# A hybrid decoder step: row scales by matmul in place of transpose, and one sample-state step in one window

## The chip, the cores and the metric
The kernel runs on one core of a Trainium2 chip. The metric is the device time of one execution in microseconds (us). The core has five engines with their own instruction streams, which meet only through semaphores: PE (TensorE, the matmul array; PEld is its weight load), DVE (VectorE), ACT (ScalarE), POOL (GpSimd) and SP (SyncE, which issues most transfers). Each stream is executed in order.

## The reference: what is computed
Two layers over a prompt of 2048 tokens of width 1024, and, apart from them, one decoding step for 8 samples that have a state each. A layer is:

```
h = rmsnorm(x) ; z = h @ w_in                 # one projection, columns split by branch
GLA:       S = diag(alpha) S + k^T v ; o = q S  ; o = rmsnorm_per_head(o) * silu(gate)
Retention: S = gamma_h S + k^T v     ; o = q S  ; o = groupnorm_per_head(o) * silu(gate)
y = x + concat(o_gla, o_ret) @ w_out
```

A final rmsnorm follows. For the prompt both recurrences are computed in chunks, as masked products of q, k and v with a carried state; for the 8 samples they are one step of the recurrence. Returned are both outputs and the four sets of states. Everything is f32.

## The kernel before
The prompt is cut in 4 blocks of 512 tokens for each of 2 layers, so there are 8 blocks n = 0 to 7. A block is cut in 4 token tiles of 128 (t), and its work in windows w = 1 to 32 of one weight slot each. Windows come in units u = (w - 1) // 4 of four slots: unit 0 is retention's q and k, 1 its v, 2 its gate, 3 is GLA's q and k, 4 its v, 5 its gate, and 6 and 7 are the output projection. Weights and activations are split in a high and a low part (`w_hi`, `w_lo`, `h_hi`, `h_lo`, `m_hi`, `m_lo`), and a product is three passes of the array: high by high, high by low, low by high. These are line L697, 24 for each window, 6 into each of four PSUM banks q = 0 to 3. ACT rounds a weight slot to `w_hi` (L257), POOL subtracts it from the slot to get `w_lo` (L264).

The order on each engine is the order in which the program text issues it. Each engine runs through the same windows, and between the products of window w and those of w + 1 come the small steps that the code assigns to window w. A wait on a semaphore holds everything behind it on that engine.

The steps that the change touches:

- **The row scales** (`scale_rows`, PE, line L383). The next block's activations are loaded already transposed, tokens along the free axis, and need the factor 1/rms of each token along that axis. POOL makes the factors `xrs` (128 x 4, L570). For each token tile, PE takes a column of `xrs`, repeated to 128 x 128, against the identity, and so writes a tile in which each row holds the 128 factors into the bank called ATT. DVE's `next_scaled` (L394) multiplies the activations by norm weight and that bank. It is done for n = 0 at the very start and for n = 1 to 3 in window 27 of the block before. Layer 2 doesn't use it.
- **The GLA state of the samples** (`sample_state_gla`, DVE, L1377). In the second block of each layer (n = 1 and n = 5, called kind 1) the states of the 8 samples lie in `ss`, two halves p of 128 x 1024. `sample_decay_gla` (L1371) multiplies both halves by alpha in window 15; the outer products k v lie in `v_b` (the first half of it is a part of the buffer `region`). Adding them is one `tensor_tensor` for each half, the first in window 16 and the second in window 17. The second signals the step V_SS[1]. PE's `sample_outputs(1)` (L802), after the products of window 17, waits for it, and so does SP, which stores the states in window 19.

The neighbours of that step on DVE, in windows 16 and 17, are `mixed(0, t)` (L1619, which waits for ACT's affine step L1229 of the same tile; that one in turn waits for a `m_lo` of POOL, L627) and the GLA q and k of window 17: L1699 twice and L1702 twice, which read the four PSUM banks of unit 3, multiply them by the decay factors and write them to `q_t` and `k_t`. Each of these frees a bank. PE's products of window 17, the first of unit 4, wait for bank q (`free_bank`, semaphore `qk_gla`) before they write it.

Windows of PE and of the other engines are not in step: DVE's steps of window 17 start as soon as the banks of unit 3 are complete, which is when PE is at the end of its window 16.

Of the kernel before, what the change touches and what calls it, by code (L numbers as in the profile page):

```python
# [25 lines left out]
TOK = 128  # L26
# [15 lines left out]
V_SP, V_SS = (8, 10), (9, 15)  # L42
# [18 lines left out]
def build(nc, d):  # L61
    f32, f32r, u8 = mybir.dt.float32, mybir.dt.float32r, mybir.dt.uint8
    ALU, ACT = mybir.AluOpType, mybir.ActivationFunctionType
    ctx = ExitStack()
    with ctx:
        def sb(name, shape, dt=f32):
            return ctx.enter_context(nc.sbuf_tensor(name, shape, dt))
# [51 lines left out]
        xrs = sb("xrs", [128, TPB])  # L119
        yrs = sb("yrs", [128, TPB])  # L120

        ident = sb("ident", [128, 128])
# [15 lines left out]
        ss = sb("ss", [128, 2, DECB, DV])  # L138
        ss_row = ss[:, :, :, :].rearrange("p i b n -> p (i b n)")
        v_b = (region[:, 1024:2048].rearrange("p (b n) -> p b n", b=DECB), sb("v_b", [128, DECB, DV])[:, :, :])  # L140
# [21 lines left out]
        P, ATT, OB, ST, X = bank[0:4], bank[4], bank[5], bank[6], bank[7]  # L162
# [213 lines left out]
        def scale_rows(pe, m):  # L376

            if m > 0:
                pe.wait_ge(rstd_x.sem, rstd_x.at(m, 1))
            for t in range(TPB):  # L380
                if m == 0 and t % 2 == 0:
                    pe.wait_ge(first_rs, t // 2 + 1)
                i = pe.transpose(ATT[:, TOK * t:TOK * t + TOK], xrs[:, t:t + 1].to_broadcast([128, 128]), ident[:, :])  # L383
            i.then_inc(ht_ps.sem, KT)

        def next_scaled(vec, m, k):
# [864 lines left out]
        def _(vec):  # L1251
# [8 lines left out]
            def step(i):  # L1260
                i.then_inc(s_v.sem, 1)
# [42 lines left out]
            for l in range(DEPTH):  # L1304
                def body(l, n, kind):
                    def done(k):
                        vec.wait_ge(s_v.sem, s_v.at(l, k))
# [15 lines left out]
                    def sample_gate():  # L1323
                        vec.wait_ge(gl_s.sem, gl_s.at(l, 3))
                        step(vec.scalar_tensor_tensor(al[:, :], X[:, 144:160], 0.0, gt[:, :], ALU.min, ALU.subtract))

                    def sample_q_ret():

                        vec.wait_ge(zt_sb.sem, zt_sb.at(l, 1))
                        apart()  # L1330
                        step(vec.stream_shuffle(rot[:, :, :], z_t[:, 0:4, :], [(p + 16) % 32 for p in range(32)]))
                        done(3)
                        vec.tensor_scalar(z_t[:, 0:2, :], z_t[:, 0:2, :], small[:, 0:1], None, ALU.mult)
                        step(vec.tensor_scalar(z_t[:, 2:4, :], z_t[:, 2:4, :], small[:, 2:3], None, ALU.mult))
                        done(4)
                        vec.scalar_tensor_tensor(rot[:, 0:2, :], rot[:, 0:2, :], small[:, 1:2], z_t[:, 0:2, :], ALU.mult, ALU.add)
                        step(vec.scalar_tensor_tensor(rot[:, 2:4, :], rot[:, 2:4, :], small[:, 3:4], z_t[:, 2:4, :], ALU.mult, ALU.add))
                        done(5)
                        for hh in range(2):
                            r = slice(64 * hh, 64 * hh + 64)  # L1340
                            vec.tensor_copy(q_s[r, 0, :, :, hh], rot[r, 0:2, :])
                        step(vec.tensor_copy(k_s[:, 0, :, :], rot[:, 2:4, :]))

                    def sample_q_gla():
                        vec.wait_ge(zt_sb.sem, zt_sb.at(l, 3))
                        for hh in range(2):
                            r = slice(64 * hh, 64 * hh + 64)
                            vec.tensor_scalar(q_s[r, 1, :, :, hh], z_t[r, 8:10, :], DK ** -0.5, None, ALU.mult)
                        step(vec.tensor_copy(k_s[:, 1, :, :], z_t[:, 10:12, :]))

                    def sample_product(g):

                        vec.wait_ge(v_in.sem, v_in.at(l, 64 * g + 64))
                        for p in range(2):
                            i = vec.tensor_tensor(v_b[p], v_b[p], k_s[:, g, p, :].unsqueeze(2).to_broadcast([128, DECB, DV]), ALU.mult)
                        step(i)

                    def sample_state_ret():

                        done(V_SP[0])  # L1360
                        vec.wait_ge(state_in, l * 64 + 32)
                        for p in range(2):
                            i = vec.scalar_tensor_tensor(ss[:, p, :, :], ss[:, p, :, :], small[:, 4 + p:5 + p], v_b[p], ALU.mult, ALU.add)
                        step(i)

                    def sample_decay_gla():

                        vec.wait_ge(state_in, l * 64 + 64)
                        vec.wait_ge(al_s.sem, al_s.at(l, 1))
                        s2 = ss[:, :, :, :].rearrange("p i b n -> p (i b) n")  # L1370
                        step(vec.tensor_tensor(s2, s2, al[:, :].unsqueeze(2).to_broadcast([128, 16, 128]), ALU.mult))  # L1371

                    def sample_state_gla(p):

                        if p == 0:
                            done(V_SS[1] - 1)
                        i = vec.tensor_tensor(ss[:, p, :, :], ss[:, p, :, :], v_b[p], ALU.add)  # L1377
                        if p == 1:
                            step(i)

                    def sample_moments(g):

# [55 lines left out]
                    def sample_residual(u):  # L1438
                        vec.wait_ge(slot_used, n * SLOTS + (4 * (6 + u) + 5 + RING))
                        c = slice(128 * u, 128 * u + 128)  # L1440
                        step(vec.tensor_tensor(xs[:, c], OB[:, 0:128], xs[:, c], ALU.add))

                    def sample_work(w):
                        if kind == 0:
                            if w == 4:
                                sample_gate()
                            if w == 8:
                                sample_q_ret()
                            if w == 19:
                                sample_q_gla()  # L1450
                        if kind == 1:
                            if w == 9:
                                sample_product(0)
                            if w == 10:
                                sample_state_ret()
                            if w == 13:
                                sample_product(1)
                            if w == 14:
                                sample_moments(0)
                            if w == 15:  # L1460
                                sample_decay_gla()
                            if w == 17:
                                sample_normed(0)
                            if w == 18:
                                sample_affine(0)
                            if w == 19:
                                sample_moments(1)
                            if w == 21:
                                sample_normed(1)
                            if w == 23:  # L1470
                                sample_affine(1)
                                sample_mixed()
                            if w == 29:
                                sample_residual(0)
                        if n % NBLK == 2:
                            if w == 8:
                                done(V_X1)
                                sample_stats(l + 1)
                            if w == 14:
                                sample_mean(l + 1)  # L1480
# [186 lines left out]
                    for w in range(1, SLOTS):  # L1667
                        if kind == 0 and w == 2:
                            clear_states()
                        if w in (3, 4):  # L1670
# [7 lines left out]
                            for p in range(2):  # L1678
                                i = vec.tensor_tensor_scan(half_la[:, p, :], keep[:, :], half_la[:, p, :], 0.0, ALU.mult, ALU.add)
                            i.then_inc(scan_sb.sem, 1)  # L1680
                            vec.wait_ge(scan_sb.sem, scan_sb.at(n, hf + 1))
                            for sgn in range(2):
                                i = vec.tensor_scalar(nb[:, :, sgn, 2 * hf:2 * hf + 2], la[:, :, 256 * hf + MID:256 * hf + 256:TOK], (2.0 * sgn - 1.0) / TAU, None, ALU.mult)
# [3 lines left out]
                        if w == 8:  # L1687
# [3 lines left out]
                            for p in range(2):  # L1691
                                i = vec.tensor_tensor(cc[:, p, 0:TPB - 1], ex[:, p, 0, TOK - 1:BLK - TOK:TOK], em[:, 1:TPB, p, 0], ALU.mult)
# [12 lines left out]
                        if w == 20:  # L1705
                            vec.wait_ge(sret_sb.sem, sret_sb.at(n, 5))
                            vec.wait_ge(sgla_sb.sem, sgla_sb.at(n, 0))
                            for p in range(2):
                                c = slice(128 * p, 128 * p + 128)
                                i = vec.tensor_scalar(s_mid[:, c], s_gla[:, c], em[:, 0, p, 0:1], None, ALU.mult)  # L1710
# [23 lines left out]
                        for g, first in ((0, 9), (1, 21)) if kind == 0 else ():  # L1734
                            t = w - first
# [5 lines left out]
                                norm(g, t - 2)  # L1741
                            if 1 <= t <= TPB:
                                stats(g, t - 1)
                        if kind == 1 and w in (16, 17):
                            sample_state_gla(w - 16)
                        if 14 <= w < 18:
                            mixed(0, w - 14)
                        if w == (2 if n == 0 else 1 if n < NBLK - 1 else 18) and n < LAST:
# [54 lines left out]
                    if n % NBLK == 2:  # L1803
                        sample_norm(l + 1)

                blocks(l, body)


# [116 lines left out]
```

## Time and profile before
| | |
|---|---|
| median of 3 runs | 1724.93 us (1724.77 to 1725.31) |
| the profiled execution | 1724.93 us |
| its span, first to last instruction | 1722.9 us |
| PE busy | 1701.6 us, 99% |
| DVE busy | 942.0 us, 55% |
| POOL busy | 842.1 us, 49% |
| ACT busy | 657.6 us, 38% |

The profile is of one execution. A row of a timeline gives start and length in us; rows of the same form that follow each other are merged (x2, x4), with the time from the first start to the last end. Starts of one engine can lie before the end of its instruction before, because an engine overlaps them: a matmul of PE with 512 columns takes 0.39 us, but the next one starts 0.23 us after it. For PE the distance between two starts is therefore the price of an instruction, and not its length. In square brackets stands the idle time ahead of an instruction and who ended it. An instruction's length on DVE or POOL includes the time for which it was held off after its issue.

### The profile page before, as it was taken

The numbers are of one execution on the slowest core, as the hardware profiler recorded it, in microseconds if no ns is written. First come the engines' busy times: TensorE is split into PE (matmuls) and PEld (weight loads), VectorE is DVE, ScalarE is ACT, GpSimd is POOL, SyncE is SP. The second block draws the span as 40 slices with busy tenths as digits, with TensorE's granted clock in tenths as the row PEclk, the third lists the DMA queues.
The fourth block names the chain that finished last, engine by engine and source line by source line (L and its number), as shares of the span: only waits on it lengthen the run. The fifth ranks groups of instructions, "written<-read, shape, count | busy, mean of one in ns | idle before, by whom it ended". The sixth has DMA issues, their size and how long they took to land.

```text
span 1722.9 us, 26529 instructions
## 1 busy us (share of the span) xinstructions
PE 1701.6 (99%) x10266; PEld 1401.0 (81%) x10266; DVE 942.0 (55%) x2284; ACT 657.6 (38%) x1287; POOL 842.1 (49%) x661
## 2 busy tenths in 40 slices
PE   6999999999999999999999999999999999999998
PEld 4888878888788887888878888788888888878886
DVE  7643566746555174464454535759556464584454
ACT  4433334333344234343452424434244343443322
POOL 4444345654455444464444544547445464454635
PEclk9999999999999999999999999999999999999999
DMA  7422356434442244322452224563244322442224
GB/s 259 135 65 84 100 207 197 147 111 145 161 137 84 86 135 159 117 86 83 136 168 88 74 74 149 184 178 128 74 150 159 111 76 85 134 157 80 86 86 140
DMA packets 100189, 215.97 MB, mean 125 GB/s; under 512 B 12896, under 2 KB 15328, under 8 KB 100064
## 3 DMA queue, kind: packets, MB, share of 16 engines
q10 hardware_dynamic: 73872, 134.51, 23.7%
q1 hardware_dynamic: 26192, 79.76, 14.2%
q8 instruction: 81, 1.33, 0.3%
q14 instruction: 44, 0.36, 0.1%
HBM read 192.34 MB, written 21.89 MB: 124 GB/s over the span
## 4 chain that ended last, share of the span: by engine, by line
PE 99%; DMA 1%; DVE 0%; issue 0%; ACT 0%; ACTq 0%; POOLq 0%; POOL 0%; SPq 0%
PE bank L697 82%; PE bank L972 2%; PE bank L1013 2%; PE bank L978 2%; PE bank L760 1%; PE bank L956 1%; PE bank L939 1%; PE bank L918 1%; PE bank L373 1%; PE bank L880 1%; PE bank L922 1%; PE bank L718 0%; PE bank L989 0%; PE bank L770 0%; PE bank L897 0%; PE bank L662 0%
## 5 line engine op out<-in xcount | busy, mean ns | idle before, releaser
L264 POOL TENSOR_TENSOR w_lo<-w_stage,w_hi 128x512 fp32r<-128x512 f32 x264 | 360.9, 1388 | 352.3 <-ACT w_hi L257 352.3
L697 PE MATMUL bank<-h_hi,w_hi 128*128 128x512 f32 x1024 | 410.2, 401 | 3.7 <-DVE h_lo L361 3.7
L697 PE MATMUL bank<-h_lo,w_hi 128*128 128x512 f32 x1024 | 400.4, 391 | 0.0
L697 PE MATMUL bank<-h_hi,w_lo 128*128 128x512 f32 x1024 | 400.2, 391 | 0.0
L264 POOL TENSOR_TENSOR w_lo<-ss,w_hi 128x512 fp32r<-128x512 f32 x164 | 216.5, 1341 | 232.4 <-ACT w_hi L257 232.4
L257 ACT ACTIVATE w_hi<-w_stage 128x512 fp32r<-128x512 f32 x264 | 152.6, 624 | 352.4 <-PE bank L697 311.0
L697 PEld LDWEIGHTS bank<-h_hi,w_hi 128*128 128x128 f32 x1024 | 192.7, 188 | 53.9 <-issue 7.2
L697 PEld LDWEIGHTS bank<-h_hi,w_lo 128*128 128x128 f32 x1024 | 192.8, 188 | 41.5
L697 PEld LDWEIGHTS bank<-h_lo,w_hi 128*128 128x128 f32 x1024 | 193.0, 189 | 37.0
L697 PE MATMUL bank<-w_hi,m_hi 128*128 128x512 f32 x512 | 203.6, 398 | 0.0
L697 PE MATMUL bank<-w_hi,h_hi 128*128 128x512 f32 x512 | 202.7, 396 | 0.0
L697 PE MATMUL bank<-w_lo,m_hi 128*128 128x512 f32 x512 | 199.6, 390 | 0.0
L697 PE MATMUL bank<-w_hi,m_lo 128*128 128x512 f32 x512 | 199.6, 390 | 0.0
L697 PE MATMUL bank<-w_hi,h_lo 128*128 128x512 f32 x512 | 199.6, 390 | 0.0
L697 PE MATMUL bank<-w_lo,h_hi 128*128 128x512 f32 x512 | 199.4, 390 | 0.0
L257 ACT ACTIVATE w_hi<-ss 128x512 fp32r<-128x512 f32 x164 | 94.6, 623 | 212.9 <-PE bank L697 177.0
L264 POOL TENSOR_TENSOR w_lo<-v_b,w_hi 128x512 fp32r<-128x512 f32 x84 | 110.5, 1336 | 124.3 <-ACT w_hi L257 124.3
L570 POOL TENSOR_TENSOR rstd<-var,half 128x4 f32<-128x4 f32 x64 | 66.4, 1038 | 131.3 <-DVE var L1594 68.0
L697 PEld LDWEIGHTS bank<-w_hi,h_hi 128*128 128x128 f32 x512 | 96.3, 188 | 20.2 <-issue 1.2
L697 PEld LDWEIGHTS bank<-w_hi,h_lo 128*128 128x128 f32 x512 | 96.1, 188 | 20.4
L697 PEld LDWEIGHTS bank<-w_hi,m_lo 128*128 128x128 f32 x512 | 96.1, 188 | 20.2
L697 PEld LDWEIGHTS bank<-w_hi,m_hi 128*128 128x128 f32 x512 | 96.2, 188 | 20.1 <-issue 0.4
(221 smaller groups left out, 2279.8 us busy)
## 6 DMA issues: line engine op xcount, KB each, us to landing
w_stage<-in_w_slots ACTq DMA_DIRECT2D x264, 256.0 KB, 3.0
ss<-in_w_slots ACTq DMA_DIRECT2D x164, 256.0 KB, 2.9
v_b<-in_w_slots ACTq DMA_DIRECT2D x84, 256.0 KB, 3.0
region<-in_x_prompt SPq DMA_DIRECT2D x32, 512.0 KB, 4.2
xn<-in_x_t SPq DMA_DIRECT2D x16, 512.0 KB, 4.3
out_acts<-region SPq DMA_DIRECT2D x16, 512.0 KB, 3.5
xn<-out_acts SPq DMA_DIRECT2D x16, 512.0 KB, 3.8
region<-out_acts SPq DMA_DIRECT2D x16, 512.0 KB, 3.4
```

The source lines that it names most:

```text
L257: nc.scalar.activation(w_hi[:, h // 2 % RING, c], stage(h), ACT.Copy).then_inc(hi_done, 1)
L264: pool.tensor_tensor(w_lo[:, r, c], stage(h), w_hi[:, r, c].bitcast(f32), ALU.subtract).then_inc(lo_done, 1)
L373: i = pe.transpose(dst[:, TOK * t:TOK * t + TOK], xn[:, t, 128 * k:128 * k + 128], ident[:, :])
L570: pool.tensor_tensor(dst, src, half[0:dst.shape[0], 0:dst.shape[-1]], ALU.pow).then_inc(s, 1)
L697: i = pe.matmul(P[q][:, :], x, y, start=(s == 0 and kk == 0 and c == 0), stop=(s == 3 and kk == 1 and c == 2), skip_group_check=True)
L760: i = pe.matmul((ST if Z_BANK[u] == "S" else X)[32 * c:32 * c + 32, 0:128], hs[:, k, :], stage(first - 2 * s + k)[:, 128 * c:128 * c + 128 ...
L880: i = pe.transpose((X, ATT)[t // 2][:, c:c + 128], k_t[:, p, TOK * t:TOK * t + TOK], ident[:, :])
L918: pe.matmul(OUT[hh][:, c], a[:, h, :], v_n[:, t, 128 * h:128 * h + 128], start=(p == 0), stop=False, skip_group_check=True)
L922: i = pe.matmul(OUT[hh][:, c], q_t[r, p, tile], s[r, c], start=False, stop=(p == 1), skip_group_check=True)
L972: pe.matmul(OUT_TWO[hh][:, c:c + 128], a_two[g][:, t % 2, h, :], v_n[:, t, 128 * h:128 * h + 128], start=(t % 2 == 0 and p == 0), stop=Fal ...
L978: i = pe.matmul(OUT_TWO[hh][:, c:c + 128], q_t[r, p, TOK * t:TOK * t + TOK], s[r, 128 * p:128 * p + 128], start=False, stop=(t % 2 == 1 an ...
L1013: i = pe.transpose(dst[:, 128 * h:128 * h + 128], o_n[:, t, 128 * h:128 * h + 128], ident[:, :])
```

## The change
`scale_rows` issues a plain matmul with the same operands in place of the transpose. `sample_state_gla` does both halves at once, in window 16; it is called from `sample_work`, which comes last in a window, and no longer from the place ahead of `mixed`.

```diff
-                i = pe.transpose(ATT[:, TOK * t:TOK * t + TOK], xrs[:, t:t + 1].to_broadcast([128, 128]), ident[:, :])
+                i = pe.matmul(ATT[:, TOK * t:TOK * t + TOK], xrs[:, t:t + 1].to_broadcast([128, 128]), ident[:, :], start=True, stop=True)
...
-                    def sample_state_gla(p):
-
-                        if p == 0:
-                            done(V_SS[1] - 1)
-                        i = vec.tensor_tensor(ss[:, p, :, :], ss[:, p, :, :], v_b[p], ALU.add)
-                        if p == 1:
-                            step(i)
+                    def sample_state_gla():
+
+                        done(V_SS[1] - 1)
+                        for p in range(2):
+                            i = vec.tensor_tensor(ss[:, p, :, :], ss[:, p, :, :], v_b[p], ALU.add)
+                        step(i)
...
+                            if w == 16:
+                                sample_state_gla()
...
-                        if kind == 1 and w in (16, 17):
-                            sample_state_gla(w - 16)
```

The new text is one line shorter, so L1619, L1699 and L1702 are L1620, L1700 and L1703 in it; L1377 keeps its number.

DVE's order in windows 15 to 17 of n = 1 before. `ss` is the sample state, `tmp` the tile of `mixed`, `bank` a PSUM bank of unit 3:

```order
L1371 TENSOR_TENSOR ss<-ss,al 128x2048
L1377 TENSOR_TENSOR ss<-ss,region 128x1024
L1619 TENSOR_TENSOR tmp<-tmp,region 128x512
L1699 SCALAR_TENSOR_TENSOR region<-bank,ex 128x512 x2
L1702 TENSOR_TENSOR region<-bank,ex 128x512 x2
L1377 TENSOR_TENSOR ss<-ss,v_b 128x1024
L1619 TENSOR_TENSOR tmp<-tmp,region 128x512
```

The same place of the same engine after the change:

```order
L1371 TENSOR_TENSOR ss<-ss,al 128x2048
L1620 TENSOR_TENSOR tmp<-tmp,region 128x512
L1377 TENSOR_TENSOR ss<-ss,region 128x1024
L1377 TENSOR_TENSOR ss<-ss,v_b 128x1024
L1700 SCALAR_TENSOR_TENSOR region<-bank,ex 128x512 x2
L1703 TENSOR_TENSOR region<-bank,ex 128x512 x2
L1620 TENSOR_TENSOR tmp<-tmp,region 128x512
```

The first half has moved behind the tile of `mixed`, and the second half from behind the four steps that free the banks to ahead of them. The same happens for n = 5. PE, ACT, POOL and SP keep their orders.

## Rows read from the trace of the kernel before

**Rows 1.** The page, part 1: busy us, share of the span, instructions.
```profile
PE 1701.6 (99%) x10266; PEld 1401.0 (81%) x10266; DVE 942.0 (55%) x2284; ACT 657.6 (38%) x1287; POOL 842.1 (49%) x661
```

**Rows 2.** The waits of PE, whole span: engine line <- releaser, us, times, longest.
```profile
PE bank L383 <- POOL xrs L570: 10.9, 2, 8.7
PE bank L697 <- DVE h_lo L361: 3.7, 1, 3.7
```

**Rows 3.** Line L972 in the whole span: duration ns min/median/max, starts, forms.
```profile
L972 PE MATMUL bank<-region,tmp x192: 272/275/275, 308.7 to 1590.8; 128*128 128x128 f32 x192
```

**Rows 4.** Timeline of PE, n = 0, window 27: start us, us taken, engine, line, operation.
```profile
213.67 0.60 PE L383 MATMUL bank<-ident,xrs 128*128 128x128 f32 x4
214.03 0.48 PE L697 MATMUL bank<-w_hi,m_hi 128*128 128x512 f32 x1
214.35 0.40 PE L697 MATMUL bank<-w_lo,m_hi 128*128 128x512 f32 x1
214.58 0.40 PE L697 MATMUL bank<-w_hi,m_lo 128*128 128x512 f32 x1
```

**Rows 5.** Timeline of PE at 308 us, the f32 matmuls of L972.
```profile
308.69 1.95 PE L972 MATMUL bank<-region,tmp 128*128 128x128 f32 x16
310.57 0.71 PE L978 MATMUL bank<-s_ret,region 64*128 64x128 f32 x8
```

**Rows 6.** Timeline of all engines, the start-up.
```profile
11.58 0.69 PE L383 MATMUL bank<-ident,xrs 128*128 128x128 f32 x2 [2.26 <-POOL xrs L570]
...
12.38 1.41 DVE L394 SCALAR_TENSOR_TENSOR xn<-xn,nw,bank 128x512 f32<-128x512 f32 x2 [1.64 <-PE bank L383]
...
13.13 0.85 ACTq L248 DMA_DIRECT2D ss<-in_w_slots  x2
...
14.09 1.15 ACT L350 ACTIVATE h_hi<-xn 128x512 fp32r<-128x512 f32 x2 [0.33 <-DVE xn L394]
...
14.75 1.10 DVE L361 TENSOR_TENSOR h_lo<-xn,h_hi 128x512 fp32r<-128x512 f32 x1 [0.96 <-ACT h_hi L350]
```

**Rows 7.** Timeline of PE, n = 1, entry into window 17.
```profile
345.80 0.48 PE L697 MATMUL bank<-w_hi,h_hi 128*128 128x512 f32 x1
```

**Rows 8.** Timeline of DVE, n = 1, windows 15 to 17.
```profile
337.57 2.28 DVE L1371 TENSOR_TENSOR ss<-ss,al 128x2048 f32<-128x2048 f32 x1
339.88 2.20 DVE L1377 TENSOR_TENSOR ss<-ss,region 128x1024 f32<-128x1024 f32 x1
342.63 1.15 DVE L1619 TENSOR_TENSOR tmp<-tmp,region 128x512 f32<-128x512 f32 x1 [0.55 <-ACT tmp L1229]
343.71 1.27 DVE L1699 SCALAR_TENSOR_TENSOR region<-bank,ex 128x512 f32<-128x512 f32 x2
...
346.25 1.21 DVE L1377 TENSOR_TENSOR ss<-ss,v_b 128x1024 f32<-128x1024 f32 x1
```

**Rows 9.** Timeline of POOL, n = 1, windows 15 to 17.
```profile
338.48 2.52 POOL L627 TENSOR_TENSOR m_lo<-tmp,m_hi 128x512 fp32r<-128x512 f32 x1
340.96 3.97 POOL L264 TENSOR_TENSOR w_lo<-w_stage,w_hi 128x512 fp32r<-128x512 f32 x2
344.90 1.29 POOL L627 TENSOR_TENSOR m_lo<-tmp,m_hi 128x512 fp32r<-128x512 f32 x1
346.41 3.91 POOL L264 TENSOR_TENSOR w_lo<-w_stage,w_hi 128x512 fp32r<-128x512 f32 x2 [0.22 <-ACT w_hi L257]
```

**Rows 10.** Timeline of ACT, n = 1, window 16.
```profile
341.10 1.51 ACT L1229 ACTIVATE tmp<-bank,parh 128x128 f32<-128x128 f32 x4 [0.17 <-POOL m_lo L627]
```

**Rows 11.** Line L1377 in the whole span: the first half, in both layers.
```profile
L1377 DVE TENSOR_TENSOR ss<-ss,region x2: 2202/2202/2203, 339.9 to 1188.6; 128x1024 f32<-128x1024 f32 x2
```

**Rows 12.** Timeline of all engines, PE's pace in the start-up.
```profile
20.82 0.59 PE L697 MATMUL bank<-h_lo,w_hi 128*128 128x512 f32 x1
...
21.25 0.40 PE L697 MATMUL bank<-h_hi,w_lo 128*128 128x512 f32 x1
```

**Rows 13.** Busy time by stretch: PE, PEld, DVE, ACT, POOL, granted clock, DMA.
```profile
1716.00:1723.00 7.00, 0.21 (x1) 0.00 (x0) 2.66 (x7) 1.87 (x2) 0.96 (x2) 0.86 0.53 210
```

## The prediction

> **What bounds the kernel now.** I read the page's busy line first: PE is busy 1701.6 us of 1722.9 (99%) while DVE is at 55% [rows 1]. Then I read PE's waits, because a wait can be read as a price only on the engine that sets the end. There are three of them in the whole span, all in the first 16 us: two before L383 (10.9 us together) and one of 3.7 us before the first L697 [rows 2]. From then on PE never idles. So two rules hold for this change: every extra array pass on PE after the start is paid in full, and every wait that is pushed onto PE is paid in full, since nothing later absorbs it. Work saved on any other engine is worth nothing unless PE waits for it, and it does not. The third view is the timeline of each engine in the two places that the change touches.
>
> **Part 1, L383: four transposes become four matmuls, in four blocks (n = 0 to 3).** Operands and sizes stay; only the transpose mode goes. How is a true f32 matmul of 128x128 with 128 columns executed? L972 is one: 96 such matmuls write from tmp in the program (6 blocks, 2 pairs, 8 each), and the trace has 192 records for them [rows 3]. So an f32 matmul is two array passes, each with its own record. The transposes have one record each: x4 per block [rows 4]. Their spacing: a merged row is as long as the starts are apart plus the last one's own time, so 16 of L972 in 1.95 with 0.275 for the last start (1.95 - 0.275) / 15 = 0.112 apart, and the last is followed by L978 after 0.20 [rows 3, 5]. The four transposes take 0.60, so they start 0.109 apart, and L697 follows the last after 0.03, 0.36 us after the first [rows 4].
> After the change a block has 8 records: 7 x 0.112 = 0.78, and a tail between 0.03 (as after the transposes) and 0.20 (as from L972 to L978), so 0.81 to 0.98 against 0.36: +0.45 to +0.62 us. The row nearest in form is L972 itself, which says 0.112 for each of four added records, 0.45, and I add a little of the tail: 0.50. Blocks 1 to 3 run it inside a stretch in which PE never waits: 3 x 0.50 = +1.5 us (ends +1.35 and +1.9). An end below nothing is excluded: the operands are the same and the passes double.
> The Trainium skill, page "TensorE: Matmul & The Clock Gate", section "Terms", calls the transpose mode four times faster for FP32. The trace has two records of 0.112 against one of 0.109, a factor of two; by the page's factor the price for each transpose would be 3 x 0.109 = 0.33 and the three blocks would cost 3.9 us in place of 1.5. I go by the rows.
>
> In block 0 the same edit stands in the start-up. The last two transposes start at 11.58, and DVE's L394 waits for them until 12.38. At the slow spacing there (two take 0.69) the added records put L394 off by about 0.43. What waits for L394 is ACT's L350, at 14.09 [rows 6]. The profile blames DVE for its last 0.33 us, but the two L394 had both ended at 13.79; ACT was issuing two DMAs until 13.98. The first L394 would end about 13.5 and the second 14.2, the second being needed by 14.6, and L361 starts at 14.75 as before. So 0 us, with 0.4 us of slack; without that cover it would cost 0.43.
>
> **Part 2: the GLA sample state.** It runs once per layer, in the second block of each (n = 1 and 5). DVE had L1377 (first half), L1619, L1699 twice, L1702 twice, L1377 (second half). Now it has L1619, both L1377, and only then L1699 and L1702. No work is added. L1699 is what frees the first PSUM bank for PE's unit 4 (window 17), which PE enters at 345.80 [rows 7]. Before, the first L1699 began at 343.71 and took 0.68 (x2 in 1.27) [rows 8], so PE had 1.4 us of slack. The question is when DVE gets to it now.
> DVE's rows must be read with POOL's. The same L1377 takes 2.20 at 339.88 and 1.21 at 346.25 [rows 8]. In the first case POOL's m_lo runs from 338.48 for 2.52, to 341.0, where the one at 344.90 takes 1.29 [rows 9]. The times fit one pattern: m_lo waited while L1371 ran (to 339.85), then took 1.16; L1377 waited for it until 341.0 and then took 1.08; the next w_lo, issued at 340.96, waited until 342.08 and took 1.16 too; L1619, issued 342.63, waited for that one until 343.2. An operation of one engine with two SBUF inputs holds the other off for its whole length, and the one that waits goes next. L1699, which reads PSUM, is not slowed: 0.6 to 0.7 each while w_lo runs until 344.9.
> The Trainium skill says so too ("SBUF — State Buffer", section "SBUF: two separate sides": the port pair shared by DVE and GpSimd is an exclusive lock, not a split of bandwidth). By a split, both running at half rate, the sum below would end about 0.3 us earlier per layer; by the lock, which these rows bear out, it stands.
>
> Step by step for n = 1, in the times of before:
> 1. L1371 ends 339.85, m_lo ends 341.0 as before, so ACT's L1229, which waited for it, starts at 341.10 again [rows 10] and L1619 can start at 342.63 as before. The hole that held the first L1377 is now idle.
> 2. POOL, no longer held off by L1377, runs the two w_lo at 340.96 and 342.2, each 1.28, to 343.45. L1619 waits for the second, runs 0.55, ends 344.0.
> 3. POOL's next m_lo has been waiting since about 343.4 and goes next: 344.0 to 345.17. The first L1377 waits, then runs 1.08: 346.25.
> 4. The second L1377 follows: 347.4. POOL's next w_lo comes only at 346.41 [rows 9], 0.16 us too late to get in between.
> 5. The first L1699 ends 0.65 later, 348.0, and PE starts at about 348.1 instead of 345.80: a wait of 2.3 us. The later banks (L1699, L1702, L1702, every 0.6 us) are ready before PE, at 1.4 us each, comes to them.
>
> The second layer meets the same hold: its first L1377, 848.7 us later, takes 2.20 again [rows 11]. So 2 x 2.3 = +4.6 us. The other side of the trade: the step that the sample's PE reads (L802) wait for was signalled at 347.46 and now comes at 347.4, and PE reads it only after window 17; nobody gains. The bounds of the wait: if POOL never got in DVE's way, L1619 would end 343.25, two L1377 345.5, L1699 346.15, a wait of 0.4; if the w_lo of 346.41 slipped in between the two L1377, 1.2 more: 3.5.
>
> **Sum.** +1.5 + 0 + 4.6 = +6.1 us. The profiled execution took 1724.93 us, with a span of 1722.9, and the median of the three is the same 1724.93. Forecast 1731.0 us.
>
> **Rivals.**
> A. The lock falls better: m_lo or w_lo loses against DVE, so the wait is 0.4 to 1.4 us a layer. For it: margins in steps 2 and 3 are tenths of a us. Against: in all four encounters of [rows 8, 9] the waiting engine went next. Sum 1.5 + 2 x 0.9 = +3.3: 1728.2, on either side of the limit.
> B. The lock falls worse: step 4 has 0.16 us of margin, the w_lo gets in. 1.5 + 2 x 3.5 = +8.5: 1733.4.
> C. No wait on PE at all, which ends not slower. The place is L1699 in window 17; it decides whether it begins by 345.1. With both L1377 (2.3 us) ahead, L1619 would have to end by 342.8, and it cannot begin before 342.4, since ACT is busy with w_hi until 340.93 and L1229 takes 1.5. Only if L1377 ran far below 1.1 us would this hold. Then only part 1 is left: +1.5, 1726.4, no measurable change.
> D. PE's clock rises sooner. L697 takes 0.59 and the next starts 0.43 later up to 21.25; from there it takes 0.40 [rows 12], and later starts are 0.23 apart [rows 4]: the lower and the higher of the two levels (1.2 and 2.4 GHz). PE had begun its steady work at about 15.9, when L361 ended [rows 6]. The matmuls at L383 put a little more work on PE ahead of that. At most the 5.3 us would go at the fast rate: 5.3 x (1 - 0.23/0.43) = 2.5 us back, +3.6, 1728.5. Against: it is 0.9 us of extra work, and there is a hole of 3.7 us behind it. The Trainium skill speaks for this one ("TensorE: Matmul & The Clock Gate", section "Part 4: PE-mode transpose": transposes do not count as PE activity for the clock gate as matmuls do); no row here shows it. The reverse, a clock that falls while PE waits 2.3 us, is held off by the end of the kernel: PE is busy for 0.21 us of the last 7 and the granted clock is 0.86 over them [rows 13], which is the lower level for the last 2.0 us only, 4.9 us after PE's last work.
>
> **How the numbers follow.** Forecast 0.62; A 0.15; B 0.10; C 0.05; D 0.06; something outside these 0.02. What a measurement of this kernel can tell is 0.2%, 3.4 us, so the limits are 1721.5 and 1728.4. Slower: the forecast, B, and half of A and D, 0.62 + 0.10 + 0.11 = 0.83. Same: the other halves and C, 0.15. Faster: 0.02, since no term is below nothing but D's. Range: from 1727.5 (A with a wait of 0.6 a layer) to 1733.6 (B).
>
> **What would show it.** L383 with 32 PE records in place of 16 and L697 0.8 to 1.0 us after the first of them. A new row in PE's waits: L697 waits for DVE's L1700 (the new number of L1699), 2 times, 4.6 us. DVE's order L1620, L1377, L1377, L1700, with the first L1377 again long (over 2 us, issued while m_lo holds it off). The start of PE's first L697 unchanged at about 16. Wrong would be: 16 records at L383 (part 1 is nothing), no wait of PE on L1700 (C), or an added wait elsewhere.

## The result, and the profile after

| | before | after |
|---|---|---|
| median | 1725.31 us (1724.77 to 1725.71, 6 runs) | 1732.83 us (1732.33 to 1737.38, 6 runs) |
| ratio after to before, 95% interval | | 1.0051 [1.0039, 1.0064] |
| the profiled execution, its span | 1724.93 us, 1722.9 | 1735.79 us, 1733.8 |

The change makes the kernel slower, as forecast, but by 0.51% and not by 0.35%. 1.0051 times the median before is 1734.1 us, above the end of the range (1733.6). The median of the six runs in the table, 1732.83, lies inside the range (1.0044 times the median before); the mean of all ten runs of the change on record, 1734.3, lies above it like the ratio. Also new: the runs no longer agree. Before, six runs lie within 0.9 us of each other; after, the six lie within 5.1 and the ten go from 1731.1 to 1737.5.

PE's waits in the trace after (same view as [rows 2]):

```profile
PE bank L383 <- POOL xrs L570: 10.5, 2, 8.8
PE bank L697 <- DVE region L1700: 5.6, 2, 3.5
PE bank L697 <- DVE h_lo L361: 3.3, 1, 3.3
PE bank L662 <- DVE xn L394: 0.5, 1, 0.5
```

The second row is the wait that the forecast named, twice in the span: on L1700, with 5.6 us in place of 4.6, and one of the two is 3.5. A wait in this view begins when the matmul ahead of it ends, so it is about 0.25 us shorter than the delay of the next start, by which the table below counts. The last row is new as well and belongs to the start-up.

The two traces hold the same PE instructions but for the 16 added records, so each can be paired with its partner. The difference of their starts grows only in these places:

| PE instruction | start before | start after | added since the row above |
|---|---|---|---|
| L662, block 0 | 24.36 | 24.56 | 0.20, start-up |
| first L697 after L383, n = 0 | 214.03 | 214.69 | 0.46, part 1 |
| first L697 of window 17, n = 1 | 345.80 | 350.15 | 3.69, wait on DVE |
| first L697 after L383, n = 1 | 422.56 | 428.98 | 2.07: part 1, and 1.6 more |
| first L697 after L383, n = 2 | 630.26 | 637.11 | 0.43, part 1 |
| first L697 of window 17, n = 5 | 1194.52 | 1203.75 | 2.38, wait on DVE |
| end of the span | 1722.9 | 1733.8 | 1.67, no wait of PE |

The sum is 10.9 us, the whole difference of the two executions. Two terms of it, 1.6 us each after a wait, have no row among PE's waits. PE's timeline right after the first wait shows them:

```profile
350.15 0.47 PE L697 MATMUL bank<-w_hi,h_hi 128*128 128x512 f32 x1 [3.46 <-DVE region L1700]
...
351.16 0.39 PE L697 MATMUL bank<-w_lo,h_hi 128*128 128x512 f32 x1
351.39 0.54 PE L697 MATMUL bank<-w_hi,h_lo 128*128 128x512 f32 x1
351.73 0.63 PE L697 MATMUL bank<-w_hi,h_hi 128*128 128x512 f32 x1
352.15 0.63 PE L697 MATMUL bank<-w_lo,h_hi 128*128 128x512 f32 x1
...
354.71 0.48 PE L697 MATMUL bank<-w_lo,h_hi 128*128 128x512 f32 x1
355.03 0.39 PE L697 MATMUL bank<-w_hi,h_lo 128*128 128x512 f32 x1
```

Read the distance between starts, not the length. It is 0.23 until 351.39, then 0.34 once and 0.43 from there on, and 0.23 again after 355.03. From 351.39 to 355.03 PE starts 9 products, which takes 3.64 us and would take 9 x 0.23 = 2.07: 1.57 us lost. It is the granted clock, as the view by stretches says (columns as in [rows 13]):

```profile
344.00:347.00 3.00, 2.69 (x14) 2.01 (x13) 3.00 (x2) 0.68 (x3) 2.11 (x2) 1.00 0.00 0
347.00:350.00 3.00, 0.00 (x0) 0.00 (x0) 3.00 (x4) 2.41 (x6) 2.94 (x2) 1.00 0.55 175
350.00:353.00 3.00, 2.85 (x9) 2.28 (x10) 3.00 (x8) 0.00 (x0) 1.79 (x2) 0.75 0.88 348
353.00:356.00 3.00, 3.00 (x11) 2.40 (x10) 0.43 (x2) 0.00 (x0) 0.00 (x0) 0.69 0.01 4
```

PE does nothing from 347 to 350; the clock is still 1.00 there, and falls only after PE has started again: 0.75 and 0.69 over the next two stretches of 3 us are 3.4 us at the lower level (3 x 0.25 / 0.5 + 3 x 0.31 / 0.5), 1.2 GHz in place of 2.4. The same happens around the wait of n = 5, behind which PE starts again at 1203.75:

```profile
1202.00:1208.00 6.00, 4.25 (x12) 3.42 (x13) 6.00 (x11) 2.33 (x6) 5.14 (x3) 0.73 0.73 265
1208.00:1214.00 6.00, 6.00 (x54) 4.52 (x54) 5.92 (x14) 2.16 (x4) 2.10 (x2) 0.98 0.27 85
```

So a wait of PE can be paid twice, once as a wait and once as slow products that follow. The page's line of clocks shows 9 in all 40 slices, and cannot show it: 3.4 us are a thirteenth of a slice.

Part 1 in the trace after, block 0 in window 27 (against [rows 4]):

```profile
213.88 1.05 PE L383 MATMUL bank<-ident,xrs 128*128 128x128 f32 x8
214.69 0.48 PE L697 MATMUL bank<-w_hi,m_hi 128*128 128x512 f32 x1
215.00 0.39 PE L697 MATMUL bank<-w_lo,m_hi 128*128 128x512 f32 x1
```

Eight records, L697 0.81 us after the first, against 0.36: +0.45, the lower end of the forecast.

Part 2, n = 1: DVE, then POOL, in the trace after (against [rows 8, 9]). This PE is 0.66 us later than in the trace before:

```profile
338.47 2.28 DVE L1371 TENSOR_TENSOR ss<-ss,al 128x2048 f32<-128x2048 f32 x1
343.54 1.42 DVE L1620 TENSOR_TENSOR tmp<-tmp,region 128x512 f32<-128x512 f32 x1 [2.79 <-ACT tmp L1229]
344.88 2.31 DVE L1377 TENSOR_TENSOR ss<-ss,region 128x1024 f32<-128x1024 f32 x1
347.12 2.29 DVE L1377 TENSOR_TENSOR ss<-ss,v_b 128x1024 f32<-128x1024 f32 x1
349.33 1.28 DVE L1700 SCALAR_TENSOR_TENSOR region<-bank,ex 128x512 f32<-128x512 f32 x2
```

```profile
338.69 3.22 POOL L627 TENSOR_TENSOR m_lo<-tmp,m_hi 128x512 fp32r<-128x512 f32 x1
341.87 2.55 POOL L264 TENSOR_TENSOR w_lo<-w_stage,w_hi 128x512 fp32r<-128x512 f32 x2
344.37 1.74 POOL L627 TENSOR_TENSOR m_lo<-tmp,m_hi 128x512 fp32r<-128x512 f32 x1
347.06 3.48 POOL L264 TENSOR_TENSOR w_lo<-w_stage,w_hi 128x512 fp32r<-128x512 f32 x2 [0.95 <-ACT w_hi L257]
```

The steps of the forecast are all there: L1620 issued 343.54 waits for the second w_lo (to 344.4), the first L1377 waits for m_lo and takes 2.31 as one of 2.20 did before. But the second takes 2.29 too: POOL's w_lo is issued at 347.06, L1377 at 347.12, and POOL goes first. That is rival B. It was due for a reason that the forecast did not have. ACT ahead of it, in the trace after:

```profile
334.52 1.75 ACTq L248 DMA_DIRECT2D w_stage<-in_w_slots  x2
335.03 0.61 ACT L257 ACTIVATE w_hi<-w_stage 128x512 fp32r<-128x512 f32 x1
336.32 1.51 ACT L1229 ACTIVATE tmp<-bank,parh 128x128 f32<-128x128 f32 x4 [0.67 <-issue]
```

The same issue in the trace before:

```profile
333.87 0.82 ACTq L248 DMA_DIRECT2D w_stage<-in_w_slots  x2
```

Issuing two transfers of weights took ACT's queue 1.75 us in place of 0.82, so L1229 started 0.7 us late, m_lo and L1371 met in another way, and everything behind was 0.2 us later: enough to use up the margin of 0.16. This is read from the traces; no experiment isolates it. Two traces taken later bear it out: in e7 and e11 below the same issue took 1.63 us, and the second L1377 kept its place ahead of w_lo, in e11 by 0.03 us (issued 347.46 against 347.49). The slow issue at this point is not a rare event either. It stands in all four traces of kernels with the matmul in every block (the change 1.75, e1 2.02, e7 and e11 1.63) and in none of the other nine, which all have 0.82. So part 1 seems to bring it about and to work on part 2 in this way, which the forecast, with its separate terms, left out; by what path is not shown. At n = 5 the issue was short, the second L1377 took 1.21, and the wait was 2.38.

### The profile page after: what moved, and what is told of

Read it like the earlier page. It is cut to its first block, busy times and chain, and to the rows that moved or that the text cites. A ratio compares the mean times of both kernels' runs of the same rounds, so it can differ in the third digit from the quotient of the medians.

```text
span 1733.8 us, 26561 instructions
## 1 busy us (share of the span) xinstructions
PE 1707.1 (98%) x10282; PEld 1405.9 (81%) x10282; DVE 942.3 (54%) x2284; ACT 657.4 (38%) x1287; POOL 839.0 (48%) x661
## 4 chain that ended last, share of the span: by engine, by line
PE 96%; DVE 1%; POOL 1%; DMA 1%; ACT 0%; issue 0%; ACTq 0%; POOLq 0%; SPq 0%
PE bank L697 80%; PE bank L972 2%; PE bank L1013 2%; PE bank L978 2%; PE bank L760 1%; PE bank L956 1%; PE bank L939 1%; PE bank L918 1%; PE bank L373 1%; PE bank L880 1%; PE bank L922 1%; PE bank L718 0%; PE bank L989 0%; PE bank L770 0%; PE bank L897 0%; DVE ss L1377 0%
## 5 line engine op out<-in xcount | busy, mean ns | idle before, releaser
L264 POOL TENSOR_TENSOR w_lo<-w_stage,w_hi 128x512 fp32r<-128x512 f32 x264 | 355.4, 1367 | 367.6 <-ACT w_hi L257 367.6
L697 PE MATMUL bank<-h_hi,w_hi 128*128 128x512 f32 x1024 | 409.9, 400 | 3.3 <-DVE h_lo L361 3.3
L697 PE MATMUL bank<-h_lo,w_hi 128*128 128x512 f32 x1024 | 400.2, 391 | 0.0
L697 PE MATMUL bank<-h_hi,w_lo 128*128 128x512 f32 x1024 | 400.0, 391 | 0.0
L697 PEld LDWEIGHTS bank<-h_hi,w_hi 128*128 128x128 f32 x1024 | 192.6, 188 | 53.4 <-issue 7.2
L697 PEld LDWEIGHTS bank<-h_hi,w_lo 128*128 128x128 f32 x1024 | 192.7, 188 | 41.3
L697 PEld LDWEIGHTS bank<-h_lo,w_hi 128*128 128x128 f32 x1024 | 192.9, 188 | 36.9
L697 PE MATMUL bank<-w_hi,h_hi 128*128 128x512 f32 x512 | 203.9, 398 | 5.6 <-DVE region L1700 5.6
L697 PE MATMUL bank<-w_hi,m_hi 128*128 128x512 f32 x512 | 203.6, 398 | 0.0
L697 PE MATMUL bank<-w_hi,h_lo 128*128 128x512 f32 x512 | 201.0, 392 | 0.0
L697 PE MATMUL bank<-w_lo,h_hi 128*128 128x512 f32 x512 | 200.7, 392 | 0.0
L697 PE MATMUL bank<-w_hi,m_lo 128*128 128x512 f32 x512 | 199.6, 390 | 0.0
L697 PE MATMUL bank<-w_lo,m_hi 128*128 128x512 f32 x512 | 199.6, 390 | 0.0
L697 PEld LDWEIGHTS bank<-w_hi,h_hi 128*128 128x128 f32 x512 | 97.0, 190 | 26.6 <-issue 7.3
L697 PEld LDWEIGHTS bank<-w_hi,h_lo 128*128 128x128 f32 x512 | 96.9, 189 | 20.6
L697 PEld LDWEIGHTS bank<-w_lo,h_hi 128*128 128x128 f32 x512 | 97.0, 189 | 19.3
L697 PEld LDWEIGHTS bank<-w_hi,m_lo 128*128 128x128 f32 x512 | 96.1, 188 | 20.3
```

The lines of the kernel that those rows point to most:

```text
L264: pool.tensor_tensor(w_lo[:, r, c], stage(h), w_hi[:, r, c].bitcast(f32), ALU.subtract).then_inc(lo_done, 1)
L697: i = pe.matmul(P[q][:, :], x, y, start=(s == 0 and kk == 0 and c == 0), stop=(s == 3 and kk == 1 and c == 2), skip_group_check=True)
```

## Experiments

Each was timed beside the kernel before on the same chip, whose medians there were 1725.19 (e1 to e4), 1725.28 (e5 to e8) and 1725.12 us (e9 to e11).

**e1: the matmul alone.** The diff's first hunk only.

> The matmul at L383 alone; the sample state as before. By the account of the two traces: 3 x 0.455 us in blocks 1 to 3, and in the start-up -0.58 (PE's clock rises 0.7 us earlier) + 0.25 (later first product) + 0.52 (a wait before L662) = +0.2, so +1.6 us, 1726.9, with the granted clock at the higher level from about 20.4 us to the end of PE's work and no wait on DVE in window 17. The rival, that the plain matmul costs more by way of something that the traces hide (a clock that falls also without a long wait): over +3 us.

Measured 1726.74 us (1726.28 to 1727.31, 11 runs), ratio 1.0008 [0.9999, 1.0017]: +1.55 us. The interval just includes 1, but the fastest of these 11 runs is slower than the slowest of the 23 of the kernel before (1725.87). There is no fall of the clock in the trace. Its PE is 0.45 us later after each of the three L383, and once more by 0.37 at window 17 of n = 1, where ACT's issue was slow again:

```profile
334.40 2.02 ACTq L248 DMA_DIRECT2D w_stage<-in_w_slots  x2
...
336.48 1.51 ACT L1229 ACTIVATE tmp<-bank,parh 128x128 f32<-128x128 f32 x4 [0.94 <-issue]
```

There even the order of before is late: L1699 starts at 345.89, where it started at 343.71. So the 1.4 us of slack are not always there, and an event on ACT's queue costs PE something by way of DVE.

**e9 and e10: the matmul in block 0 alone, and in blocks 1 to 3 alone.**

```diff
+                if m == 0:        # e9; m > 0 in e10
+                    i = pe.matmul(ATT[:, TOK * t:TOK * t + TOK], ..., start=True, stop=True)
+                else:
+                    i = pe.transpose(ATT[:, TOK * t:TOK * t + TOK], ..., ident[:, :])
```

> The matmul at L383 in block 0 (the start-up) alone, no other change. If the added passes are covered there, as L361 waits for POOL's w_lo and ACT anyway: within 0.3 us of the kernel before, wherever the rise of the clock falls in the start-up, since a PE that is faster there only meets DVE's L394 before L662. If they are not covered: +0.4 us. If the plain matmuls bring the clock up earlier to any effect: up to 2.5 us faster.

> The matmul at L383 in blocks 1 to 3 alone, no other change: 3 x 0.455 = 1.37 us, and 0 to 0.4 us more where the later entry of PE or a slow issue of a transfer on ACT makes the order of POOL and DVE ahead of window 17 worse; 1726.6 to 1726.9. If three blocks cost less than 1.0, the spacing of the records in the trace is not their price.

Measured: e9 1725.05 us (1724.81 to 1725.38), -0.07, ratio 1.0000 [0.9991, 1.0009]; e10 1726.50 us (1726.21 to 1726.84), +1.38, ratio 1.0008 [0.9999, 1.0016], with all its runs above all those of the kernel before (1725.51 at most). Part 1 is 3 x 0.455 = 1.37 and the start-up is free; the 0.20 in the account above is the variation of one execution. Here is e9's start-up (all engines; L397 is L394 of before, L384 the matmul):

```profile
11.50 1.22 PE L384 MATMUL bank<-ident,xrs 128*128 128x128 f32 x4 [1.73 <-POOL xrs L573]
...
12.83 1.41 DVE L397 SCALAR_TENSOR_TENSOR xn<-xn,nw,bank 128x512 f32<-128x512 f32 x2 [2.17 <-PE bank L384]
...
14.03 1.15 ACT L350 ACTIVATE h_hi<-xn 128x512 fp32r<-128x512 f32 x2 [0.38 <-issue]
...
14.70 1.09 DVE L361 TENSOR_TENSOR h_lo<-xn,h_hi 128x512 fp32r<-128x512 f32 x1 [0.46 <-ACT h_hi L350]
```

DVE's L397 is later than L394 in [rows 6] and L361 is not, as forecast. Rival D is gone too: PE's products come at 0.24 apart from 19.35 us on in e9 (matmuls), from 19.53 in e2 and from 21.25 in the kernel before (both transposes), from 21.4 in e1 (matmuls). Over the 13 traces the earliest is 19.25 (e3) and the latest 22.15 (e4), both with transposes, so the time of the rise does not follow L383. An early rise gains nothing: there PE meets DVE before L662 (0.6 to 1.0 us in e2, e3 and e5), since DVE's L394 sets the pace. A late one costs little: 0.26 us in e4's trace.

**e2: the sample state alone.** The diff's other hunks.

> The sample state in window 16 alone; L383 stays a transpose. By the account: two waits of PE before the first product of window 17, each 2.4 us where DVE gets the second L1377 in ahead of POOL's w_lo, or 3.7 where POOL goes first, and 1.57 us more for each time that the granted clock falls to the lower level after such a wait. 4.8 to 10.5 us, likeliest 6 to 9, with runs that differ from each other by steps of 1.2 to 1.6 us. The rival (the clock falls only because of the plain matmuls): 4.8 to 6, with no fall of the clock and all runs within 0.5 us.

Measured 1731.51 us (1731.32 to 1732.93), ratio 1.0038 [1.0025, 1.0052], +6.3. Its trace has two waits of 2.38 to 2.40 (by the starts of PE), 4.8, and one fall of the clock, after the second (its PE starts again at 1199.37):

```profile
1197.00:1200.00 3.00, 0.86 (x6) 0.58 (x4) 3.00 (x5) 2.96 (x7) 2.40 (x2) 1.00 0.62 223
1200.00:1203.00 3.00, 3.00 (x10) 2.36 (x9) 3.00 (x5) 0.00 (x0) 2.75 (x2) 0.57 0.79 307
1203.00:1206.00 3.00, 3.00 (x13) 2.44 (x12) 3.00 (x8) 0.00 (x0) 0.00 (x0) 0.86 0.00 0
```

4.78 + 1.57 = 6.35, which is the measured difference. All five runs have a mean clock of 0.998 or 0.997, against 0.999 or 1.000 in the kernel before; a fall of 3.4 us at half the clock takes 0.001 off the mean (3.4 x 0.5 / 1729), so each run had at least one. The rival, that the clock falls only because of the plain matmuls, is refuted: there are none here.

**e4: PE kept at work during the wait.** As e2, and:

```diff
+                        if kind == 1 and w == 17:
+                            pe.wait_ge(od_sb.sem, od_sb.at(l, 1))
+                            for _ in range(16):
+                                pe.transpose(ATT[:, 0:128], ident[:, :], ident[:, :])
                         unit_slot(u, s)
```

> As the kernel with the sample state alone in window 16, and PE is given 16 more transposes of the identity (0.109 us each, 1.75 us in all, result not used) ahead of window 17 in the second block of each layer, in the time in which it would wait. If the clock falls because PE stands idle, it stays up here: only the waits themselves are left, 4.8 to 7.4 us over the kernel before, and runs close to each other; 1.6 to 3.1 us under the kernel with the state alone. If the fall has another cause (the load on the chip at that moment), it is still there and the time is that of the kernel with the state alone. The waits shown by PE would be 0.7 to 2 us each.

Measured 1729.91 us (1729.68 to 1730.31), ratio 1.0027 [1.0017, 1.0038], +4.72. PE at window 17, n = 1, and the clock:

```profile
346.29 1.91 PE L1032 MATMUL bank<-ident 128*128 128x128 f32 x16
348.59 0.47 PE L697 MATMUL bank<-w_hi,h_hi 128*128 128x512 f32 x1 [0.39 <-DVE region L1704]
```

```profile
346.00:349.00 3.00, 2.61 (x23) 2.36 (x21) 3.00 (x5) 2.88 (x7) 2.17 (x2) 1.00 0.56 190
349.00:352.00 3.00, 3.00 (x15) 2.48 (x14) 3.00 (x6) 0.19 (x1) 2.99 (x2) 1.00 0.85 337
352.00:355.00 3.00, 3.00 (x43) 2.28 (x41) 0.85 (x4) 0.62 (x2) 0.00 (x0) 1.00 0.00 0
```

L697 starts 2.38 us later than it would without waiting, exactly as in e2: DVE decides that, and the filling costs nothing. But no fall of the clock is left in either layer, the runs lie within 0.6 us, and the kernel with 32 more instructions is 1.6 us faster than e2. 2 x 2.38 = 4.76 is the whole of what is left. All seven runs are at a mean clock of 0.999 or 1.000. So the clock fell because PE stood idle. The filling is made of transposes alone, and they kept the clock up: in this kernel transposes did count as work of PE for the clock, and rival D had built on the opposite.

**e7: the whole change, with the same filling.**

> The whole change, and the 16 more transposes (result not used) ahead of window 17 in the second block of each layer. The falls of the clock are to be gone: 1725.2 + 1.5 (part 1) + two waits of 2.4 or 3.7 = 1731.5 to 1734.1, each run at one of the steps 1.3 apart, and below the whole change without them by 1.5 us or more in the mean. The rival (the falls come from part 1 and part 2 together, whatever PE does meanwhile): no gain over the whole change, 1732.8 and runs up to 1737.

**e11: the whole change again.**

> The whole change once more, beside the kernels above on one chip, for the spread of its runs: by the account 1725.2 + 1.5 + 4.8 = 1731.5 for a run with no fall of the clock, 1.57 more for each fall, 1.3 more for each layer in which POOL's w_lo gets ahead of the second L1377; so 1731 to 1737.5, and the longer the lower the mean granted clock (0.999 to 0.996).

Measured: e7 1731.37 us (1731.05 to 1732.62), ratio 1.0037 [1.0024, 1.0049]; e11 1733.44 us (1732.56 to 1736.76), ratio 1.0054 [1.0040, 1.0068]. They ran on different chips; each against its own kernel before, they are +6.1 and +8.3. The filled kernel does what the forecast said of the change itself, +6.1 us. The 15 runs of the change as it is, in both places, go from 1731.09 at a mean clock of 0.999 over 1732.3 to 1733.4 at 0.999 to 0.998 and 1734.8 to 1735.9 at 0.997 to 1736.8 to 1737.5 at 0.996; e7's runs are all at 0.999. By the 0.001 of e2's account these are no fall to three falls. The run at 1731.09 is what the forecast said. One run of e7, 1732.62, stands 1.2 us or more above the other four at the same mean clock, about the size of rival B in one layer (1.3); it was not traced. e11's trace has one fall, at PE's restart (349.41; the clock is 0.56 over 349 to 352 and 0.87 over 352 to 355), waits of 2.53 and 2.40, and one more of 0.5 on DVE's L1644 at 48.6 us, which no other trace has.

**e3: only the first half of the state moves.** `sample_state_gla(0)` last in window 16, `sample_state_gla(1)` where it was.

> L383 stays a transpose. Only the first half of the sample state moves, behind the tile of mixed in window 16; the second half stays where it was, behind L1702. DVE has one L1377 of 1.2 us ahead of L1699 in place of two. If POOL and DVE hold each other off (w_lo before L1619, m_lo before L1377), the first L1699 ends 1.1 us after PE reaches window 17: two waits of 1.1 to 1.3 us, +2.2 to +2.6 us. If they don't, L1699 ends before PE gets there: 0. The clock: waits this short should leave it up; if it falls, 1.57 more for each.

Measured 1727.60 us (1727.39 to 1728.00), ratio 1.0014 [1.0005, 1.0023], +2.41, waits of 1.26 and 1.24. The first L1377 takes 2.31 us there, held off by m_lo; at the 1.21 us that it takes alone, a wait of 0.1 to 0.2 us would be left (an estimate, 1.26 - 1.10). The clock stays up in all 11 runs (mean 0.999 or 1.000).

**e5: both halves ahead of `mixed`.** In window 16, `sample_state_gla()` before `mixed(0, 2)`.

> L383 stays a transpose. Both halves of the sample state in window 16, but ahead of the tile of mixed. By the rule that POOL and DVE hold each other off and the waiting one goes next, in the times of the kernel before: first L1377 ends 342.08, w_lo 343.24, second L1377 344.3, the other w_lo 345.5, L1619 346.1, first L1699 346.7: PE waits 0.9 to 1.0 us in each layer, +1.8 to +2.0 us, 1727.1, and the clock stays up. Without holding off: second L1377 ends 342.2, L1619 at 343.2, no wait, +0.

Measured 1727.03 us (1726.68 to 1727.50), ratio 1.0010 [1.0001, 1.0019], +1.75; waits of 0.98 and 0.97. DVE and POOL in its trace, n = 1, 0.25 us later than in the trace before:

```profile
340.14 2.21 DVE L1377 TENSOR_TENSOR ss<-ss,region 128x1024 f32<-128x1024 f32 x1
342.27 2.31 DVE L1377 TENSOR_TENSOR ss<-ss,v_b 128x1024 f32<-128x1024 f32 x1
344.50 1.77 DVE L1618 TENSOR_TENSOR tmp<-tmp,region 128x512 f32<-128x512 f32 x1
```

```profile
341.23 4.50 POOL L264 TENSOR_TENSOR w_lo<-w_stage,w_hi 128x512 fp32r<-128x512 f32 x2
```

Every second operation waits for one of the other engine: L1377, w_lo, L1377, w_lo, L1618, in turns, which is why the three of DVE take 2.21, 2.31 and 1.77 and POOL's pair 4.50 where it takes 2.55 alone. The expectation was computed with this rule alone.

**e8: one hold taken away.** As e2, without POOL's m_lo of window 16 in the second block of each layer (a part of the output projection's low terms is left out):

```diff
+                                if kind == 1 and w == 16:
+                                    pool.memset(spare[:, 31:32], 0.0).then_inc(mlo_sb.sem, 1)
+                                    continue
                                 pool.tensor_tensor(m_lo[...], tmp[...], m_hi[...], ALU.subtract).then_inc(mlo_sb.sem, 1)
```

> The sample state alone in window 16, L383 a transpose, and POOL's m_lo of window 16 is left out in the second block of each layer (a small memset stands in its place, so one tile of the output projection's low part is that of another block). If that m_lo holds off the first L1377, the wait of PE falls from 2.4 by the 1.16 us of it to 1.2 to 1.3 in each layer, no fall of the clock is left, and the time is 1725.2 + 2.5 = 1727.7, against 1731.5 with it. If L1377 is long for a reason of its own, it stays at 2.3 us, PE's waits at 2.4 and the time at 1730 or more.

Measured 1727.52 us (1727.28 to 1727.95), ratio 1.0014 [1.0005, 1.0022], +2.24; waits of 1.27 and 1.27. DVE, n = 1 (L1380 is L1377 of before):

```profile
342.45 1.41 DVE L1623 TENSOR_TENSOR tmp<-tmp,region 128x512 f32<-128x512 f32 x1 [2.79 <-ACT tmp L1232]
343.79 1.22 DVE L1380 TENSOR_TENSOR ss<-ss,region 128x1024 f32<-128x1024 f32 x1
344.92 1.21 DVE L1380 TENSOR_TENSOR ss<-ss,v_b 128x1024 f32<-128x1024 f32 x1
346.06 1.28 DVE L1703 SCALAR_TENSOR_TENSOR region<-bank,ex 128x512 f32<-128x512 f32 x2
```

The first half takes 1.22 in place of 2.31, since the engine that held it off has nothing to do; L1623 ahead of it, which still meets w_lo, takes 1.41. Half of each wait was POOL's m_lo. The Trainium skill's rule ("SBUF — State Buffer", section "SBUF: two separate sides": an exclusive lock, held for the whole instruction) agrees with every meeting of the two engines in the rows shown here.

**e6: both halves behind the banks.** In window 17, `sample_state_gla()` after L1699 and L1702, before `mixed(0, 3)`.

> L383 stays a transpose. Both halves in one window, but in window 17 behind L1699 and L1702, which free the banks. If the place relative to these is all that matters, PE waits for nothing: the second half ends at about 349.8 in the times of before, PE reads the states at 351.45; within 0.3 us of the kernel before. If doing both halves in one go costs by itself (a later tile of mixed, a later store), +1 us or more.

Measured 1725.24 us (1724.84 to 1725.64), ratio 1.0000 [0.9991, 1.0009], and PE has only the three waits of the kernel before. Both halves in one window cost nothing; what costs is their place ahead of the steps that free the banks. No experiment gave a version that is faster than the kernel before.

## Why the prediction was wrong, step by step

- **What bounds the kernel, and that every wait of PE is paid in full: right, and too weak.** A wait of 2.4 us costs 2.4, and in some executions 1.57 more (e2 against e4).
- **Part 1, +1.5: right.** Two records for each f32 matmul, 0.455 a block (forecast 0.45 to 0.62, taken 0.50), e10 measured +1.38. The factor of four of the Trainium skill ("TensorE: Matmul & The Clock Gate", section "Terms") would have given 3.9; the traces have two records for one, a factor of two.
- **Start-up, 0: right.** e9 -0.07: L394 came 0.45 us later and L361 did not.
- **Part 2, the wait of 2.3 a layer: right where the order falls as in the steps.** 2.38 in e2, e4 and at n = 5 of the change. The cause, POOL and DVE holding each other off, is shown by e8 (one hold less, 1.1 us less wait) and e5.
- **Rival B, 0.10 for both layers: undervalued for one.** The margin of 0.16 us in step 4 was named, but not what could use it: a slow issue on ACT's queue, 1.75 in place of 0.82, two engines away. It came in the profiled execution and added 1.3 us there; that the slow issue at this point stands only in traces with the whole of part 1 (4 of 4, against 0 of 9) could not be seen in the trace of before.
- **The step that failed** is the last sentence of rival D: that a falling clock "is held off by the end of the kernel". From one case, in which the clock fell 4.9 us after PE's last work, I took that idle time of 2.3 us would be let pass. The traces show otherwise: after a wait of 2.4 us (e2, n = 5) or 3.7 us (n = 1 of the change) the clock fell 1.1 and 1.3 us after PE had started again, and in e11 just as it started. The 4.9 us at the end of the kernel were one draw, not a limit: at the same place the other twelve traces have 2.1 (e7) to 5.2 us (e6). In the four falls at a wait the clock came down 2.2 to 4.8 us after PE had stopped, in the same range, and in three of the four PE was at work again by then. The term left out of the sum is 0 to 3 falls of 1.57 us. With one, 6.1 + 1.6 = 7.7, 1732.6, the forecast would have met the median of the six; the mean of the ten, 1734.3, is two falls above the fastest run (1731.1 + 3.1).
- **The range** ended at the worst case of the waits and had no room for a run-to-run term, which is where it was missed.

Not every wait brings a fall: of the traced ones, n = 5 of the change and of e2 and n = 1 of the change and of e11 did, n = 1 of e2 and n = 5 of e11 did not, though as long (2.4 us) as that of e2, n = 5. None of the waits of 1.0 to 1.3 us (e3, e5, e8) did. What decides between two equal waits was not tried, nor how three falls come about in the slowest runs, which were not traced; nor why ACT's issue is slow at times.

## What to carry to other kernels

On an engine that never waits, allow for a new wait twice: the wait, and for PE the slow products that may follow it, at 0.20 us for each product of 512 columns until the clock is back. They came with waits of 2.4 us and more here and with none of 1.3 or less; between the two nothing was tried. When you move a step on a shared in-order engine, look first for the steps behind it that free a resource of the bounding engine, and keep those ahead, as e6 does. And where DVE and POOL both work on SBUF, write their operations with two inputs in SBUF as one alternating queue before you add up durations. Ask also of each part of a change whether it moves the margins of the other, as the matmul did here.

## What the runs showed of the hardware

- The granted clock of PE fell for about 3.4 us at the end of a wait of 2.4 to 3.7 us, or 1.1 to 1.3 us behind it (2.2 to 4.8 us after PE had stopped), and not in every execution; 1.75 us of transposes within the wait kept it up (e4, e7).
- Where it rises in the start-up varies by almost 3 us between traces (19.25 us in e3 to 22.15 in e4), with 0.26 us of effect on the time at most.
- Issuing two loads of a weight slot took ACT's queue 0.82 us mostly, but 1.63 to 2.02 ahead of L1371 of n = 1 in the four traces with the matmul in every block (and about as long at some other places of every trace), and held its next activation by up to 0.94 us (e1).
